# A conditioning product's sum over partitions: from two one-column TensorE products to 32x32 block transposes, row sums and one small product

## The chip, the cores and the metric

The kernel runs as one program on 1 core of one Trainium2 chip. The metric is the device time of one execution in microseconds (us); lower is better. The median of 3 runs of the kernel before is 2657.59 us (2654.68 to 2659.80).

## What is computed

Two transformer blocks in a row over 256 tokens of width 2048, all in float32. The first block has a gated delta-rule branch, a block attention branch and a gated feed-forward part; the second has a differential attention layer and a forgetting attention layer. What the change touches is the *conditioning* of the second block: a vector `c` gives shifts, scales and gates by three matrix-vector products.

```
def second_block(x, c, w_mod, b_mod, ..., kv_w_mod, kv_b_mod, ...):
    c_act = jax.nn.silu(c)                       # (1, 2048)
    for l in range(2):
        mod = c_act @ w_mod[l] + b_mod[l]        # (1, 2048) @ (2048, 6144)
        shift, scale, gate = jnp.split(mod, 3, axis=-1)
        h = x * (1.0 + scale[:, None]) + shift[:, None]
        ...
        x = layer_norm(DN_ALPHA * x + gate[:, None] * y, ln_g[l], ln_b[l])

def shared_kv(x, c_act, w_mod_kv, b_mod_kv, ...):
    mod = c_act @ w_mod_kv + b_mod_kv            # (1, 2048) @ (2048, 4096)
    ...
```

Together these products have 6144 + 6144 + 4096 = 16384 output columns, which is 32 chunks of 512 columns.

## The kernel before, in words

**The main line.** Sixteen large matrix products (`PLAN`: "qkv", "spill", "branch", "w_out", "ffn", "down", "v2" and so on) run one after the other. Each is cut into bodies, each body into units, 820 units in the loops in all. In one unit SyncE loads 512 KB of weights (`load`, L460) into a ring of 4 slots, ScalarE rounds them to float32r (`split`, L1254: `w_hi`), VectorE subtracts to get the remainder (`split`, L1858: `w_lo`), and TensorE does 12 products of 512 columns (L631 to L633, in `chunk`: operand high by weights high, high by low, low by high) or 24 of 256 columns (L654 to L656, in `across_chunk`). The counters `hi_done`, `lo_done` and `w_used` tie the engines together: ScalarE rounds the next slot when TensorE has used it.

**The conditioning product beside it.** One chunk of 512 columns takes 16 units of a body. In unit k SyncE loads a 128 x 512 piece of the conditioning weights (L484) and VectorE, behind its `split`, multiplies it by `c_act[:, k]` and adds it to `gemv_acc` (`gemv`, L1883; L1874 for k = 0). So after 16 units `gemv_acc` (128 x 512) holds, on each of the 128 partitions, a part of the sum, and what is left is the sum over partitions. Before, in unit k = 15, VectorE does the last step twice: once into `gemv_hi`, rounded to float32r (L1881), and once into `gemv_acc` (L1883); then it subtracts to get `gemv_lo` (L1888). Five units into the next body with a chunk (`mod_due` with lag 5), TensorE sums over partitions with a stationary column of ones, `ones_r[:, 0:1]`: two products of 512 columns, one for each half (`mod_reduce`, L664 and L665). The product "branch" has no chunk; the last chunk's sum is taken at the start of "g2". Two units later ScalarE copies the 1 x 512 row out of PSUM (`mod_copy`, L1279) and issues its DMA to `mods` in DRAM (L1282). `mods` is read back in two places, hundreds of us apart.

Waits around it: VectorE waits for `mod_stored` of the chunk before ahead of L1881 (`gemv_row` shares the bytes of `gemv_lo`); TensorE waits for `gemv_cut` (both halves written) in `mod_reduce`; ScalarE waits for `mod_sum`. The order on each engine is written out by hand.

**Work of other kinds between the units.** In "spill" (L631 to L633 with `u_hi`, `u_lo`) a generator `delta_net` puts the small products of the delta rule between units. One of these, L771 (`sums` <- `pick[:, ...]`, `sq`), is a plain float32 product with a stationary operand of 128 x 16; it is used for comparison below. Two others are L1165 (ones 128 x 128 times 2 columns) and L1221 (two transposes of 16 x 128 to 128 x 16). A plain float32 product shows in the trace as two MATMUL records, each with its LDWEIGHTS; a transpose or a float32r product as one.

Of the kernel before, what the change touches and what calls it, by code (L numbers as in the profile page):

```python
# [18 lines left out]
F32 = mybir.dt.float32  # L19
F32R = mybir.dt.float32r  # L20
ALU = mybir.AluOpType
ACT = mybir.ActivationFunctionType
AX = mybir.AxisListType
ds = bass.ds

P = 128
# [3 lines left out]
KD = D // P  # L30
# [6 lines left out]
H2 = 8  # L37
H3 = 16
COLS = 512
RING = 4  # L40
RMS_EPS = 1e-6
EPS = 1e-5
# [8 lines left out]
IDENT, ONES, CAUSAL, DIST = 0, 128, 256, 384  # L51
# [61 lines left out]
def block_kernel(nc, x, norm_mix_w, w_in, conv_w, a_log, dt_bias, gdn_o_norm_w, q_norm_w, k_norm_w,  # L113
# [5 lines left out]
    with ctx:  # L119

        at = [16512]

        def place(name, shape, dtype, offset=None):
            nbytes = 4 * int(np.prod(shape[1:]))
            if offset is None:
                offset = at[0]
                at[0] += (nbytes + 31) // 32 * 32
            return nc.alloc_sbuf_tensor_at(name, list(shape), dtype, offset=offset)

        raw = place("raw", [P, RING, 2, COLS], F32)  # L130
        w_hi = place("w_hi", [P, RING, 2, COLS], F32R)
        w_lo = place("w_lo", [P, RING, 2, COLS], F32R)
        xs = place("xs", [P, HALVES, D], F32)
        keep = place("keep", [P, KEEP_W], F32)
        cols = place("cols", [P, 3 * P], F32)
        modc = place("modc", [P, P], F32)
        small = place("small", [P, 464], F32)
        stage = place("stage", [P, 2, HALVES, COLS], F32)
        gemv_w = place("gemv_w", [P, 2, COLS], F32)
        gemv_acc = place("gemv_acc", [P, COLS], F32)  # L140
        gemv_hi = place("gemv_hi", [P, COLS], F32R)

        gemv_row = place("gemv_row", [P, COLS], F32, at[0])
        gemv_lo = place("gemv_lo", [P, COLS], F32R)
        ones_r = place("ones_r", [P, 2], F32R)
        region = at[0]
        K8 = 8 * 1024

# [116 lines left out]
        def sm(col, n=1, p0=0, p1=P):  # L265
            return small[p0:p1, col:col + n]
# [25 lines left out]
        ident = keep[:, IDENT:IDENT + P]  # L292
# [4 lines left out]
        bank = [ctx.enter_context(nc.psum_tensor(f"bank{b}", [P, COLS], F32)) for b in range(8)]  # L297
# [8 lines left out]
        mods = nc.dram_tensor("mods", (MOD_COLS // P, P), F32).ap()  # L306
# [41 lines left out]
        gemv_cut = sem("gemv_cut")  # L348
        gemv_step, mod_sum, mod_copied, mod_stored = sem("gemv_step"), sem("mod_sum"), sem("mod_copied"), sem("mod_stored")
# [3 lines left out]
        def signal(name):  # L353
            if name not in S:
                S[name] = sem(name)
            return S[name]
# [25 lines left out]
        for name, bodies, units, turns in PLAN:  # L382
            pr = products[name] = Product()
# [64 lines left out]
        def _(sp):  # L448
# [5 lines left out]
            def load(pr, i, j, w, pair, col):  # L454

                if not (isinstance(i, int) and pr.unit0 + i * pr.units + j < RING):

# [124 lines left out]
        def _(pe):  # L582
# [77 lines left out]
            def mod_reduce(n, b=MODB):  # L660


                pe.wait_ge(gemv_cut, n * 2 + 2)
                pe.matmul(bank[b][0:1, :], ones_r[:, 0:1], gemv_hi[:], start=True, stop=False)  # L664
                pe.matmul(bank[b][0:1, :], ones_r[:, 0:1], gemv_lo[:], start=False, stop=True).then_inc(mod_sum, 1)  # L665

            def mod_due(pr, i, j):

# [72 lines left out]
                    thin(ws_hi, ws_lo, u_hi, u_lo).then_inc(signal("logits"), 1)  # L741

            across_body("qkv", 0, u_hi, u_lo, first_due, {q: q + 1 for q in range(8)})
            pe.wait_ge(signal("ones_ready"), 1)
            for i in range(1, products["qkv"].bodies):
                across_body("qkv", i, u_hi, u_lo)

# [234 lines left out]
            pr = products["spill"]  # L982
# [6 lines left out]
            pr = products["branch"]  # L989
# [57 lines left out]
            pr = products["ffn"]  # L1047
# [144 lines left out]
            pr = products["v3"]  # L1192
# [51 lines left out]
        def _(act):  # L1244
# [31 lines left out]
            def mod_copy(n, b=MODB):  # L1276

                act.wait_ge(mod_sum, n + 1)
                act.copy(gemv_row[0:1, :], bank[b][0:1, :]).then_inc(mod_copied, 1)  # L1279
                act.wait_ge(mod_copied, n + 1)  # L1280
                dst = mods[ds(n * 4, 4), :].rearrange("r c -> (r c)").unsqueeze(0)
                act.dma_start(dst, gemv_row[0:1, :]).then_inc(mod_stored, 16)  # L1282

            def mod_due(pr, i, j):
                m = mod_part(pr, i, j, 7)
# [46 lines left out]
            def first_due(j):  # L1332
                if j in (1, 2):
                    operand_high(2 * j + 2)
                    operand_high(2 * j + 3)
                if j == 6:
                    act.wait_ge(signal("keep_in"), 16)
                    act.copy(ones_r[:], keep[:, ONES:ONES + 2]).then_inc(signal("ones_ready"), 1)
                    act.wait_ge(signal("ws_in"), 16)
                    act.wait_ge(signal("ws_zero"), 1)  # L1340
                    act.copy(ws_hi[:, :, 0:H1], ws_raw[:, :, 0:H1])
                    act.copy(ws_hi[:, :, 32:32 + H1], ws_raw[:, :, H1:2 * H1]).then_inc(signal("ws_high"), 1)
                if j == 8:
                    act.wait_ge(signal("cols_ready"), 1)
                    act.activation(c_act, cols[:, C_VEC:C_VEC + KD], ACT.Silu).then_inc(signal("c_ready"), 1)
# [221 lines left out]
            pr = products["spill"]  # L1567
# [8 lines left out]
            pr = products["branch"]  # L1576
# [42 lines left out]
            pr = products["ffn"]  # L1619
# [231 lines left out]
        def _(dve):  # L1851
# [8 lines left out]
            def gemv(pr, i, j):  # L1860

                if without_mod(pr, i):
                    return
                part = pr.units // pr.mods
                m, k = j // part, j % part
                if k >= KD:
                    return
                n = pr.mod0 + m
                c_k, w_k = c_act[:, k:k + 1], gemv_w[:, k % 2]
                dve.wait_ge(gemv_landed[k % 2], i * (pr.mods * 8 * KD) + (n * 8 * KD + 16 * (k // 2 + 1)))  # L1870
                if k == 0:
                    if not (isinstance(i, int) and i * pr.mods + n == 0):
                        dve.wait_ge(gemv_cut, i * (pr.mods * 2) + 2 * n)
                    dve.tensor_scalar(gemv_acc[:], w_k, c_k, None, ALU.mult).then_inc(gemv_step, 1)  # L1874
                    return
                dve.wait_ge(gemv_step, i * (pr.mods * KD) + (n * KD + k))
                if k == KD - 1:
                    if not (isinstance(i, int) and i * pr.mods + n == 0):

                        dve.wait_ge(mod_stored, i * (pr.mods * 16) + 16 * n)  # L1880
                    dve.scalar_tensor_tensor(out=gemv_hi[:], in0=w_k, scalar=c_k, in1=gemv_acc[:], op0=ALU.mult,  # L1881
                                             op1=ALU.add).then_inc(gemv_cut, 1)
                dve.scalar_tensor_tensor(out=gemv_acc[:], in0=w_k, scalar=c_k, in1=gemv_acc[:], op0=ALU.mult,  # L1883
                                         op1=ALU.add).then_inc(gemv_step, 1)
                if k == KD - 1:
                    dve.wait_ge(gemv_step, i * (pr.mods * KD) + (n * KD + KD))
                    dve.wait_ge(gemv_cut, i * (pr.mods * 2) + (2 * n + 1))
                    dve.tensor_tensor(gemv_lo[:], gemv_acc[:], gemv_hi[:].bitcast(F32), ALU.subtract).then_inc(gemv_cut, 1)  # L1888

            def body(name, i, drain, between=None, limit=UNITS, finish=None):  # L1890

# [75 lines left out]
            def first_due(j):  # L1967
                if j in (1, 2):
                    operand_low(2 * j + 2)
                    operand_low(2 * j + 3)  # L1970
                if j == 5:
                    dve.wait_ge(signal("cols_sum"), 1)
                    for n, r in enumerate(ROWS_USED):
                        first = 0 if n else KD
                        ins = dve.tensor_copy(cols[:, n * P + first:n * P + r], bank[SPARE][:, n * P + first:n * P + r])
                    ins.then_inc(signal("cols_ready"), 1)
                    dve.wait_ge(signal("cols_ready"), 1)
                if j == 6:
                    dve.tensor_scalar(sm(QNS), cols[:, QN_W:QN_W + 1], SCALE, None, ALU.mult)
                    for n in range(2):  # L1980
                        dve.tensor_tensor(sm(LAM + n), cols[:, LAMS + 2 * n:LAMS + 2 * n + 1],
                                          cols[:, LAMS + 2 * n + 1:LAMS + 2 * n + 2], ALU.mult)
                if j == 7:
                    dve.wait_ge(signal("ws_high"), 1)
                    dve.tensor_tensor(ws_lo[:, :, 0:H1], ws_raw[:, :, 0:H1], ws_hi[:, :, 0:H1].bitcast(F32), ALU.subtract)
                    dve.tensor_tensor(ws_lo[:, :, 32:32 + H1], ws_raw[:, :, H1:2 * H1], ws_hi[:, :, 32:32 + H1].bitcast(F32),
                                      ALU.subtract).then_inc(signal("ws_split"), 1)
# [311 lines left out]
            pr = products["branch"]  # L2299
# [55 lines left out]
            pr = products["ffn"]  # L2355
# [79 lines left out]
            pr = products["down"]  # L2435
# [321 lines left out]
```

## Time and profile before

| what | value |
|---|---|
| median of 3 runs | 2657.59 us (2654.68 to 2659.80) |
| the profiled execution's own time | 2654.59 us |
| its span, first to last instruction | 2652.8 us |
| mean granted TensorE clock | 0.992 of 2.4 GHz |
| PE (matmul) busy | 2586.1 us, 97% |
| DVE (VectorE) busy | 1796.1 us, 68% |
| ACT (ScalarE) busy | 1171.8 us, 44% |
| HBM | 227 GB/s mean over the span |

PE is TensorE's matmul side, PEld its weight loads, which overlap the matmuls. A matmul's duration in the trace (some 400 ns for 512 columns) holds its way through the array, so two that follow each other overlap; what one costs the engine is the distance between starts. The engine of the bottleneck is seen from its idle time, not from the share of busy time alone.

### The profile page before, as it was taken

How to read it: one execution, taken by the hardware profiler on the slowest of the kernel's cores; microseconds unless marked ns; L12 is line 12 of the kernel's file. 1: busy time of each engine (PE TensorE's matmuls, PEld its weight loads, DVE VectorE, ACT ScalarE, POOL GpSimd, SP SyncE). 2: the span in 40 equal slices, each digit the busy share in tenths (PEclk: the TensorE clock that was granted, in tenths of full speed). 3: DMA queues.
4: the chain of work that ended last, by engine and by line, in shares of the span. 5: the costliest groups of instructions: out<-in, count | busy, mean ns of one | idle time of the engine just before them, and what ended most of it. 6: DMA issues, size and time to landing. Idle time of an engine off the chain costs nothing.

```text
span 2652.8 us, 38762 instructions
## 1 busy us (share of the span) xinstructions
PE 2586.1 (97%) x14614; PEld 2175.5 (82%) x14614; DVE 1796.1 (68%) x2331; ACT 1171.8 (44%) x1475; POOL 0.2 (0%) x4
## 2 busy tenths in 40 slices
PE   8999999998999999999999999999999999999997
PEld 8977777777788778888887888899987778999885
DVE  6787676775567777777776666766786665545655
ACT  4454333454344544444443334333486344335642
POOL 0000000000000000000000000000000000000000
PEclk9999999999999999999999999999999999999998
DMA  7667676875768788888887777888845556665363
GB/s 209 195 234 249 218 229 208 276 254 192 250 209 269 260 270 269 275 274 271 272 275 246 251 249 254 278 273 272 252 141 182 181 167 183 182 215 165 123 224 125
DMA packets 313837, 604.69 MB, mean 228 GB/s; under 512 B 26670, under 2 KB 28724, under 8 KB 312028
## 3 DMA queue, kind: packets, MB, share of 16 engines
q1 hardware_dynamic: 301628, 571.59, 67.2%
q10 hardware_dynamic: 12064, 31.10, 3.2%
q8 instruction: 99, 1.62, 0.2%
q14 instruction: 46, 0.38, 0.0%
HBM read 591.98 MB, written 10.62 MB: 227 GB/s over the span
## 4 chain that ended last, share of the span: by engine, by line
PE 74%; DVE 2%; ACT 2%; issue 1%; DMA 1%; ACTq 0%; DVEq 0%; SPq 0%
PE bank L631 18%; PE bank L633 18%; PE bank L632 18%; PE bank L654 5%; PE bank L656 5%; PE bank L655 5%; PE bank L593 1%; PE bank L1091 1%; DVE w_lo L1858 1%; ACT w_hi L1254 0%; DMA raw<-in_w_branch_gdn 0%; PE bank L1102 0%; PE bank L1112 0%; PE bank L1088 0%; PE bank L1114 0%
## 5 line engine op out<-in xcount | busy, mean ns | idle before, releaser
L1858 DVE TENSOR_TENSOR w_lo<-raw,w_hi 128x1024 fp32r<-128x1024 f32 x820 | 1001.4, 1223 | 802.1 <-ACT w_hi L1254 801.0
L1254 ACT CAST w_hi<-raw 128x1024 fp32r<-128x1024 f32 x820 | 859.9, 1050 | 1371.7 <-PE bank L633 1028.2
L631 PE MATMUL bank<-w_hi,u_hi 128*128 128x512 f32 x1216 | 493.8, 406 | 3.1 <-DVE u_lo L1917 2.2
L632 PE MATMUL bank<-w_lo,u_hi 128*128 128x512 f32 x1216 | 483.8, 398 | 0.0
L633 PE MATMUL bank<-w_hi,u_lo 128*128 128x512 f32 x1216 | 483.2, 397 | 0.0
L1883 DVE SCALAR_TENSOR_TENSOR gemv_acc<-gemv_w,small,gemv_acc 128x512 f32<-128x512 f32 x480 | 357.8, 745 | 5.6 <-DMA gemv_w<-in_w_mod 5.2
L631 PE MATMUL bank<-w_hi,s_hi 128*128 128x512 f32 x768 | 311.1, 405 | 1.2 <-DVE w_lo L1858 1.1
L633 PE MATMUL bank<-w_hi,s_lo 128*128 128x512 f32 x768 | 304.6, 397 | 0.0
L632 PE MATMUL bank<-w_lo,s_hi 128*128 128x512 f32 x768 | 304.4, 396 | 0.0
L654 PE MATMUL bank<-s_hi,w_hi 128*128 128x256 f32 x1024 | 289.5, 283 | 0.0
L655 PE MATMUL bank<-s_lo,w_hi 128*128 128x256 f32 x1024 | 288.3, 282 | 0.0
L656 PE MATMUL bank<-s_hi,w_lo 128*128 128x256 f32 x1024 | 288.3, 282 | 0.0
L631 PEld LDWEIGHTS bank<-w_hi,u_hi 128*128 128x128 f32 x1216 | 230.3, 189 | 65.6 <-issue 8.1
L633 PEld LDWEIGHTS bank<-w_hi,u_lo 128*128 128x128 f32 x1216 | 230.3, 189 | 56.2
L632 PEld LDWEIGHTS bank<-w_lo,u_hi 128*128 128x128 f32 x1216 | 230.6, 190 | 51.5
L655 PEld LDWEIGHTS bank<-s_lo,w_hi 128*128 128x128 f32 x1024 | 193.2, 189 | 0.3
L656 PEld LDWEIGHTS bank<-s_hi,w_lo 128*128 128x128 f32 x1024 | 193.2, 189 | 0.0
L654 PEld LDWEIGHTS bank<-s_hi,w_hi 128*128 128x128 f32 x1024 | 192.0, 187 | 0.7 <-issue 0.3
L633 PEld LDWEIGHTS bank<-w_hi,s_lo 128*128 128x128 f32 x768 | 144.9, 189 | 35.3
L631 PEld LDWEIGHTS bank<-w_hi,s_hi 128*128 128x128 f32 x768 | 144.9, 189 | 34.8 <-DVE w_lo L1858 1.5
L632 PEld LDWEIGHTS bank<-w_lo,s_hi 128*128 128x128 f32 x768 | 145.2, 189 | 32.7
L631 PE MATMUL bank<-w_hi,hid_hi 128*128 128x512 f32 x352 | 140.0, 398 | 0.0
(356 smaller groups left out, 2903.5 us busy)
## 6 DMA issues: line engine op xcount, KB each, us to landing
gemv_w<-in_w_mod SPq DMA_DIRECT2D x384, 256.0 KB, 3.0
raw<-in_w_in SPq DMA_DIRECT2D x176, 512.0 KB, 4.5
raw<-in_a_w_in SPq DMA_DIRECT2D x128, 512.0 KB, 4.5
raw<-in_w_ffn_gate SPq DMA_DIRECT2D x88, 512.0 KB, 4.5
raw<-in_w_ffn_up SPq DMA_DIRECT2D x88, 512.0 KB, 4.1
raw<-in_w_ffn_down SPq DMA_DIRECT2D x88, 512.0 KB, 4.0
gemv_w<-in_kv_w_mod SPq DMA_DIRECT2D x128, 256.0 KB, 3.6
raw<-in_kv_w SPq DMA_DIRECT2D x64, 512.0 KB, 3.7
```

The lines of the kernel that those rows point to most:

```text
L593: ins = pe.transpose(b[:, f * T + th * P:f * T + (th + 1) * P], src(f, th), ident)
L631: pe.matmul(o, xh, w_hi[:, s, t], start=(k == 0), stop=False)
L632: pe.matmul(o, xh, w_lo[:, s, t], start=False, stop=False)
L633: ins = pe.matmul(o, xl, w_hi[:, s, t], start=False, stop=(k == 2 * units - 1))
L654: pe.matmul(o, wh, hi[:, k], start=(k == 0 and f % 2 == 0), stop=False)
L655: pe.matmul(o, wh, lo[:, k], start=False, stop=False)
L656: ins = pe.matmul(o, wl, hi[:, k], start=False, stop=(k == 2 * half - 1 and f % 2 == 1))
L1091: ins = pe.matmul(b[:, P:3 * P], queries_of[p][:, a, P:T], k_t[:, a, 0:T], start=True, stop=not mask)
L1254: act.copy(w_hi[:, s], raw[:, s]).then_inc(hi_done, 1)
L1858: dve.tensor_tensor(w_lo[:, s], raw[:, s], w_hi[:, s].bitcast(F32), ALU.subtract).then_inc(lo_done, 1)
L1883: dve.scalar_tensor_tensor(out=gemv_acc[:], in0=w_k, scalar=c_k, in1=gemv_acc[:], op0=ALU.mult, op1=ALU.add).then_inc(gemv_step, 1)
```

## The change

The split of `gemv_acc` into two float32r halves goes. In unit k = 15 VectorE does the last step once, transposes each 32 x 32 block of the 128 x 512 accumulator (`gemv_t`) and sums each run of 32 columns (`gemv_sums`, 128 x 16). Now partition 32a + j holds, in column b, the sum over the 32 partitions of quadrant a for the output column 32b + j. TensorE adds the four quadrants: one plain float32 product with `gemv_sums` (128 x 16) as the stationary operand and `quads` (128 x 32, a 1 where p mod 32 = column) as the moving one gives a 16 x 32 result, the chunk's 512 columns in order. `quads` is made once, from the identity, in unit 6 of the first body, by a VectorE row sum; the ScalarE copy that made `ones_r` there goes. ScalarE's copy and the DMA to `mods` handle 16 rows of 32 in place of 1 row of 512. VectorE's wait for `mod_stored` now stands before the row sum, behind the transpose. The small tiles take 2368 bytes a partition instead of 4128, so what is placed behind them moves down by 1760 bytes.

```
-        gemv_hi = place("gemv_hi", [P, COLS], F32R)
-
-        gemv_row = place("gemv_row", [P, COLS], F32, at[0])
-        gemv_lo = place("gemv_lo", [P, COLS], F32R)
-        ones_r = place("ones_r", [P, 2], F32R)
+        gemv_t = place("gemv_t", [P, COLS], F32)
+        gemv_sums = place("gemv_sums", [P, COLS // SQ], F32)
+        gemv_row = place("gemv_row", [P, SQ], F32)
+        quads = place("quads", [P, SQ], F32)
...
                 pe.wait_ge(gemv_cut, n * 2 + 2)
-                pe.matmul(bank[b][0:1, :], ones_r[:, 0:1], gemv_hi[:], start=True, stop=False)
-                pe.matmul(bank[b][0:1, :], ones_r[:, 0:1], gemv_lo[:], start=False, stop=True).then_inc(mod_sum, 1)
+                pe.matmul(bank[b][0:COLS // SQ, 0:SQ], gemv_sums[:], quads[:], start=True, stop=True).then_inc(mod_sum, 1)
...
-            pe.wait_ge(signal("ones_ready"), 1)
+            pe.wait_ge(signal("quads_ready"), 1)
...
                 act.wait_ge(mod_sum, n + 1)
-                act.copy(gemv_row[0:1, :], bank[b][0:1, :]).then_inc(mod_copied, 1)
+                act.copy(gemv_row[0:COLS // SQ], bank[b][0:COLS // SQ, 0:SQ]).then_inc(mod_copied, 1)
                 act.wait_ge(mod_copied, n + 1)
-                dst = mods[ds(n * 4, 4), :].rearrange("r c -> (r c)").unsqueeze(0)
-                act.dma_start(dst, gemv_row[0:1, :]).then_inc(mod_stored, 16)
+                dst = mods[ds(n * 4, 4), :].rearrange("r (q c) -> (r q) c", c=SQ)
+                act.dma_start(dst, gemv_row[0:COLS // SQ]).then_inc(mod_stored, 16)
...
-                if k == KD - 1:
-                    if not (isinstance(i, int) and i * pr.mods + n == 0):
-
-                        dve.wait_ge(mod_stored, i * (pr.mods * 16) + 16 * n)
-                    dve.scalar_tensor_tensor(out=gemv_hi[:], in0=w_k, scalar=c_k, in1=gemv_acc[:], op0=ALU.mult,
-                                             op1=ALU.add).then_inc(gemv_cut, 1)
                 dve.scalar_tensor_tensor(out=gemv_acc[:], in0=w_k, scalar=c_k, in1=gemv_acc[:], op0=ALU.mult,
                                          op1=ALU.add).then_inc(gemv_step, 1)
                 if k == KD - 1:
                     dve.wait_ge(gemv_step, i * (pr.mods * KD) + (n * KD + KD))
+                    dve.transpose(gemv_t[:], gemv_acc[:]).then_inc(gemv_cut, 1)
                     dve.wait_ge(gemv_cut, i * (pr.mods * 2) + (2 * n + 1))
-                    dve.tensor_tensor(gemv_lo[:], gemv_acc[:], gemv_hi[:].bitcast(F32), ALU.subtract).then_inc(gemv_cut, 1)
+                    if not (isinstance(i, int) and i * pr.mods + n == 0):
+                        dve.wait_ge(mod_stored, i * (pr.mods * 16) + 16 * n)
+                    dve.tensor_reduce(gemv_sums[:], gemv_t[:].rearrange("p (b c) -> p b c", c=SQ), AX.X, ALU.add).then_inc(
+                        gemv_cut, 1)
...
                 if j == 6:
+                    dve.wait_ge(signal("keep_in"), 16)
+                    dve.tensor_reduce(quads[:], ident.rearrange("p (q c) -> p c q", c=SQ), AX.X, ALU.add).then_inc(
+                        signal("quads_ready"), 1)
```

TensorE around the fourth chunk's sum, in "spill", before (the names behind the arrow are moving and stationary operand; the sizes are the output's):

```order
L633 MATMUL bank<-w_hi,u_lo 128x512
L664 MATMUL bank<-gemv_hi,ones_r 1x512
L665 MATMUL bank<-gemv_lo,ones_r 1x512
L631 MATMUL bank<-w_hi,u_hi 128x512
L632 MATMUL bank<-w_lo,u_hi 128x512
```

and after the change:

```order
L633 MATMUL bank<-w_hi,u_lo 128x512
L664 MATMUL bank<-quads,gemv_sums 16x32
L631 MATMUL bank<-w_hi,u_hi 128x512
L632 MATMUL bank<-w_lo,u_hi 128x512
```

Two instructions of 512 columns became one of 32, in the same place between the same neighbours.

VectorE in the last unit of the third chunk, before:

```order
L1858 TENSOR_TENSOR w_lo<-raw,w_hi 128x1024
L1881 SCALAR_TENSOR_TENSOR gemv_hi<-gemv_w,small,gemv_acc 128x512
L1883 SCALAR_TENSOR_TENSOR gemv_acc<-gemv_w,small,gemv_acc 128x512
L1888 TENSOR_TENSOR gemv_lo<-gemv_acc,gemv_hi 128x512
L1858 TENSOR_TENSOR w_lo<-raw,w_hi 128x1024
```

and after the change:

```order
L1855 TENSOR_TENSOR w_lo<-raw,w_hi 128x1024
L1874 SCALAR_TENSOR_TENSOR gemv_acc<-gemv_w,small,gemv_acc 128x512
L1878 STREAM_TRANSPOSE gemv_t<-gemv_acc 128x512
L1882 TENSOR_REDUCE gemv_sums<-gemv_t 128x16
L1855 TENSOR_TENSOR w_lo<-raw,w_hi 128x1024
```

Three instructions stay three, in the same place; two of them are of other kinds.

## Rows read from the trace of the kernel before

**Rows 1.** The page: busy time by engine; the granted clock in 40 slices.
```profile
PE 2586.1 (97%) x14614; PEld 2175.5 (82%) x14614; DVE 1796.1 (68%) x2331; ACT 1171.8 (44%) x1475; POOL 0.2 (0%) x4
...
PEclk9999999999999999999999999999999999999998
```

**Rows 2.** Busy time in stretches (us: length, busy us of each engine, clock, DMA).
```profile
160.00:700.00 540.00, 520.35 (x3388) 408.02 (x3386) 369.39 (x486) 240.84 (x310) 0.00 (x0) 0.98 0.72 237
700.00:1910.00 1210.00, 1204.15 (x5982) 1002.35 (x5983) 856.07 (x976) 499.47 (x536) 0.00 (x0) 1.00 0.80 261
```

**Rows 3.** Timeline, PE, around one chunk's sum (start us, duration us, engine, line).
```profile
376.99 0.40 PE L633 MATMUL bank<-w_hi,u_lo 128*128 128x512 f32 x1
377.22 0.40 PE L664 MATMUL bank<-gemv_hi,ones_r 128*1 128x512 f32 x1
377.46 0.40 PE L665 MATMUL bank<-gemv_lo,ones_r 128*1 128x512 f32 x1
377.69 0.39 PE L631 MATMUL bank<-w_hi,u_hi 128*128 128x512 f32 x1
```

**Rows 4.** Timeline, weight loads: of L664, and of L771.
```profile
376.99 0.08 PEld L664 LDWEIGHTS bank<-gemv_hi,ones_r 128*1 128x1 f32 x1
...
178.93 1.41 PEld L771 LDWEIGHTS bank<-sq,pick 128*16 128x16 f32 x8 [0.36 <-issue]
180.76 0.19 PEld L631 LDWEIGHTS bank<-w_hi,u_hi 128*128 128x128 f32 x1 [0.42 <-issue]
```

**Rows 5.** Timeline, PE, before and behind eight records of L771.
```profile
178.61 0.39 PE L633 MATMUL bank<-w_hi,u_lo 128*128 128x512 f32 x1
...
179.81 1.03 PE L771 MATMUL bank<-sq,pick 128*16 128x256 f32 x4
180.76 0.51 PE L631 MATMUL bank<-w_hi,u_hi 128*128 128x512 f32 x1
181.11 0.39 PE L632 MATMUL bank<-w_lo,u_hi 128*128 128x512 f32 x1
```

**Rows 6.** The instructions of L771 (count; duration ns min/median/max).
```profile
L771 PE MATMUL bank<-sq,pick x32: 376/379/518, 173.5 to 194.6; 128*16 128x256 f32 x32
```

**Rows 7.** Timeline, PE, around L1165.
```profile
1628.75 0.39 PE L633 MATMUL bank<-w_hi,hid_lo 128*128 128x512 f32 x1
1628.98 0.28 PE L1165 MATMUL bank<-small,keep 128*128 128x2 f32 x2
1629.12 0.48 PE L631 MATMUL bank<-w_hi,s_hi 128*128 128x512 f32 x1
1629.43 0.40 PE L632 MATMUL bank<-w_lo,s_hi 128*128 128x512 f32 x1
```

**Rows 8.** Timeline, PE, around L1221.
```profile
2257.66 0.29 PE L655 MATMUL bank<-s_lo,w_hi 128*128 128x256 f32 x1
2257.78 0.27 PE L656 MATMUL bank<-s_hi,w_lo 128*128 128x256 f32 x1
2257.99 0.29 PE L1221 MATMUL bank<-keep,zf_sb 16*128 16x16 f32 x2
2258.21 0.39 PE L654 MATMUL bank<-s_hi,w_hi 128*128 128x256 f32 x1
2258.43 0.28 PE L655 MATMUL bank<-s_lo,w_hi 128*128 128x256 f32 x1
```

**Rows 9.** Timeline, PE: what follows three of the 32 sums.
```profile
189.07 1.04 PE L771 MATMUL bank<-sq,pick 128*16 128x256 f32 x4
...
251.39 0.80 PE L897 MATMUL bank<-early,inv_t 64*64 64x64 f32 x20 [1.18 <-DVE inv_t L2225]
...
884.48 0.50 PE L631 MATMUL bank<-w_hi,u_hi 128*128 128x512 f32 x1 [2.15 <-DVE u_lo L1917]
```

**Rows 10.** Groups by line and shape, DVE (busy us, mean ns | idle before, releaser).
```profile
L1881 DVE SCALAR_TENSOR_TENSOR gemv_hi<-gemv_w,small,gemv_acc 128x512 fp32r<-128x512 f32 x32 | 23.9, 745 | 0.1
L1888 DVE TENSOR_TENSOR gemv_lo<-gemv_acc,gemv_hi 128x512 fp32r<-128x512 f32 x32 | 22.1, 692 | 2.2
L1874 DVE TENSOR_SCALAR gemv_acc<-gemv_w,small 128x512 f32<-128x512 f32 x32 | 15.4, 480 | 0.0
L2157 DVE TENSOR_REDUCE small<-work 128x1 f32<-128x256 f32 x32 | 13.1, 409 | 0.0
L2090 DVE TENSOR_REDUCE small<-o_sq 128x8 f32<-128x1024 f32 x2 | 2.4, 1206 | 0.0
```

**Rows 11.** Timeline, DVE: a reciprocal of 16 x 256; the last chunk's last instruction.
```profile
198.23 1.73 DVE L2069 RECIPROCAL gates<-gates 16x256 f32<-16x256 f32 x1
...
1911.08 0.69 DVE L1888 TENSOR_TENSOR gemv_lo<-gemv_acc,gemv_hi 128x512 fp32r<-128x512 f32 x1
```

**Rows 12.** Timeline, weight loads: the last chunk's sum.
```profile
1912.45 0.09 PEld L664 LDWEIGHTS bank<-gemv_hi,ones_r 128*1 128x1 f32 x1
```

**Rows 13.** Who waited for whom, DVE and ACT (us in total, times, longest us).
```profile
ACT w_hi L1254 <- PE bank L633: 1028.2, 567, 7.5
DVE w_lo L1858 <- ACT w_hi L1254: 801.0, 652, 6.1
```

More of the change, by code:

```diff
@@ L39 @@
 COLS = 512
+SQ = 32
 RING = 4
@@ L1336, in first_due @@
                 if j == 6:
-                    act.wait_ge(signal("keep_in"), 16)
-                    act.copy(ones_r[:], keep[:, ONES:ONES + 2]).then_inc(signal("ones_ready"), 1)
                     act.wait_ge(signal("ws_in"), 16)
```

## The prediction

> **What bounds the kernel now.** I read the page first: PE is busy 97% of the span, DVE 68%, ACT 44%, and the granted clock is at 0.9 or more of 2.4 GHz in all slices but the last [rows 1]. Then the stretches: from 700 to 1910 us, where 23 of the 32 chunks' sums lie (the 24th is at 1912), PE is busy 1204 of 1210 us, from 160 to 700 us, where the other eight lie, 520 of 540 [rows 2]. Then who waits for whom: the long waits are those of ACT for PE, 1028 us, and of DVE for ACT, 801 us [rows 13]. So TensorE sets the pace and hands it to the others; a microsecond taken from TensorE's stream is a microsecond of the kernel, unless TensorE has to stand right behind it, and work on VectorE or ScalarE costs nothing until it makes TensorE wait. That is why most of the working is about what one small product costs in the midst of TensorE's stream, and it has to be taken from distances between starts, since durations overlap.
>
> **What TensorE loses.** From L633 to the next L631 around a sum are 0.70 us, three steps of 0.233 us; two of them are L664 and L665 [rows 3]. Removed: 0.466 us a chunk, times 32 = 14.9 us.
>
> **What TensorE gains.** One plain float32 product, stationary operand 128 x 16, 32 columns. The trace has no such product of 32 columns, but it has L771 with the same stationary shape and 256 columns. From L633 to L632 around eight records of L771 are 181.11 - 178.61 = 2.50 us [rows 5]. Without them it would be two steps, 0.466, so they insert 2.03 us. Four of them take 1.03 us with one duration of 0.38 in it [rows 5, 6], so a record's step is (1.03 - 0.38) / 3 = 0.217 us, eight are 1.73, and 0.30 us is left over. The reason can be seen: the first weight load of L771 does not start behind the product before it, as that of L664 does (at 376.99, together with L633), but 0.32 us after L633's start, with an idle time before it that nothing in the profile explains, and the L631 that follows again loads late, 0.42 us idle [rows 4]. TensorE empties on both sides, at 0.32 - 0.23 = 0.09 us on entering, and then the first two weight loads of the large products are not hidden. The new product has two records, each 32/256 of 0.217 = 0.027 us. Inserted: 0.30 + 0.05 = 0.35 us a chunk. Net: 0.466 - 0.354 = 0.11 us, times 32 = 3.6 us.
>
> The bounds of this term come from two other small products. L1165 has a stationary operand of the full 128 x 128 and 2 columns: 1629.43 - 1628.75 = 0.68 us against 0.466, so it inserts 0.21 us; its weight load is early, nothing empties [rows 7]. By that the gain would be 0.25 us a chunk, 8.0 us. L1221, two transposes with 16 of 128 rows in use, stands among products of 256 columns, whose step is 0.12: 2258.43 - 2257.78 = 0.65 against 0.24, so 0.41 inserted, with two weight loads of 128 columns that ours does not have [rows 8]. By that the gain is 0.05 us a chunk, 1.7 us. I take L771's, since its form and its stationary shape are those of the new product.
>
> The Trainium skill, page "TensorEngine Tiling (Array Packing)", section "Key Properties", says that going from one tiling mode to another drains TensorE, with no price. L771's rows agree, at 0.30 us in all; L664's, whose stationary operand has one column, do not, as its weights load early [rows 4]. If the rule held for narrow products of every type, the pair removed would have paid as well and the gain would be up to 32 x 0.30 = 9.6 us more; the rows exclude that.
>
> **Corrections for neighbours.** Behind the first chunk's sum L771 follows at once [rows 9]: it pays the switch already, so 0.3 us more is gained there. Behind two others TensorE stands, 1.18 us for `inv_t` and 2.15 us for `u_lo` [rows 9], both from VectorE work released by products before the sum; their 0.1 us each goes into the wait. Together +0.1.
>
> **VectorE.** Removed a chunk: L1881, 0.745, and L1888, 0.692, in all 1.44 us. Added: a block transpose and a row sum of 128 x 512. The row sum is bounded by 0.41 for 256 columns and 1.21 for 1024; between them 1.04 ns a column, so 0.67 us [rows 10]. The transpose is not in the trace: from below 0.48 (L1874, the fastest pass over 128 x 512), from above the slowest per column that there is, a reciprocal of 256 columns at 1.73, so 3.5 for 512 [rows 10, 11]. I take 0.69, that of L1888, one plain pass, which is nearest in kind. Together 1.36 against 1.44: the same. The Trainium skill, page "Vector Engine (DVE) Microarchitecture Reference", section "The reshape front-end and per-opcode configuration", has the transpose sustain one element per cycle and lane; no row here shows it. The same skill's "VectorE: DVE Perf Modes", section "Rules for kernel authors", calls the row sum the slowest operation and advises restructuring; at 0.41 us for 256 columns it is no slower here than the 0.69 for 512 that it replaces, and neither would move TensorE.
>
> Who waits: the sums are ready five units ahead of TensorE's turn, some 14 us, except for the last chunk. There `gemv_lo` ends at 1911.77 [rows 11] and L664's weights load at 1912.45 [rows 12], a margin of 0.68 us; with the new pair the end is within 0.1 us of that. The wait for `mod_stored`, behind which the row sum and the next `split` are queued, is for a store issued eight units earlier, some 20 us. One row sum of some 0.3 us in unit 6 of the first body lies in VectorE's idle time [rows 13].
>
> **ScalarE, the DMA, the layout.** The copy of 16 x 32 in place of 1 x 512 can only be shorter, the store has 16 pieces of 128 bytes instead of one of 2048 and is read hundreds of us later; ScalarE waits 1028 us for TensorE [rows 13]. Nothing. Of the move by 1760 bytes no row says anything; nothing, with a spread in the range.
>
> **Sum.** 3.6 + 0.1 = 3.7 us less. The profiled execution's own time is 2654.59, so its like would be 2650.9; it stands 3.0 under the median of the runs, 2657.59, against which I predict 2653.9. What a measurement of this kernel tells from no change is 0.2%, 5.3 us, so this is the case "same", near its edge.
>
> **Rivals.**
> 1. *No emptying: the product costs what L1165's rows say.* For it: L664, which is as narrow, loads early [rows 4]. Against it: L664 is float32r, and L771, plain float32 and 128 x 16 like the new product, does not. Gain 8.0 us: 2649.6, faster. 15%.
> 2. *The transpose is slow.* If it takes 3.5 us, VectorE's chunk end grows by 2.7. TensorE then waits for it at the last chunk (2.7 - 0.7 = 2.0 us), and in the stretch from 160 to 700, where VectorE carries the delta rule's chain and TensorE already stands 20 us [rows 2], half of it may come through at each of eight chunks, 11 us. Less the 3.7 gained: +9, 2667, slower. In the 23 chunks between it hides in VectorE's idle time (354 of 1210 us). It cancels the gain from about 1.7 us a transpose on, and is over 0.2% from about 2.8 on. Against it: no pass over 512 columns in the trace takes over 0.75 us but for division. 12%.
> 3. *Stalls and clock fall otherwise.* The stretch from 160 to 700 and the one behind 1910 have waits between three engines, and the clock stood at 0.98 in the first [rows 2]; a shift of some tenths may lengthen or shorten these by 2 or 3 us. Either side, 2648 to 2660. 10%.
>
> **Chances.** The sum as worked out has 63%. Of that, with a spread of some 3 us from execution to execution (the three runs lie 5 us apart), 17 points fall beyond 0.2% faster, 44 within, 2 slower. Rival 1: 11 faster, 4 within. Rival 2: 8 slower, 4 within. Rival 3: 4 faster, 3 within, 3 slower. Sum: faster 0.32, same 0.55, slower 0.13. The range: 2647 takes in rival 1 with some spread; 2661 takes in a transpose of middling cost and L1221's price with the runs' spread. The likeliest case alone has 2650 to 2658.
>
> **What would show it.** Right: L664 (the new product) in two records per chunk, its first weight load about 0.32 us after L633's start with idle time before it, and about 0.82 us from that L633 to the second large product behind (0.47 + 0.35; before, four steps, 0.93). Wrong by rival 1: the weight load starts together with L633 and the same distance is about 0.68. Wrong by rival 2: the transpose's row says over 1.5 us, and TensorE waits for it at the last chunk. VectorE's busy time should be within 3 us of 1796, ScalarE's some 10 us lower, and the stretch from 900 to 1390 us, free of waits, shorter by 0.11 us for each of its sums.

## The result, and the profile after

| | us | runs |
|---|---|---|
| before | 2657.06 (2654.68 to 2659.80) | 4 |
| after | 2636.34 (2634.68 to 2636.89) | 4 |
| ratio | 0.9925, 95% interval 0.9913 to 0.9936 | |

The change gives 20.7 us, where 3.7 were forecast. The time lies 10.7 us below the low end of the range, and the case was called "same": the prediction was wrong. Below, 3.8 to 4.5 us of the gain turn out to be the sums, as forecast, and some 16 us to be the one item that was costed at nothing, the move of everything behind the small tiles.

The page of the changed kernel, first and clock lines:

```profile
span 2634.8 us, 38761 instructions
...
PE 2567.4 (97%) x14614; PEld 2169.4 (82%) x14614; DVE 1797.9 (68%) x2332; ACT 1157.7 (44%) x1474; POOL 0.2 (0%) x4
...
PEclk9999999999999999999999999999999999999998
```

The clock is as before [rows 1]. VectorE is 1.8 us busier, ScalarE 14.1 us less, TensorE 18.7 us less.

**The sum itself came out as forecast.** Timeline of PE and then of the weight loads around the chunk's sum near 925 us (start, duration, engine, line):

```profile
924.67 0.40 PE L633 MATMUL bank<-w_hi,u_lo 128*128 128x512 f32 x1
925.00 0.23 PE L664 MATMUL bank<-quads,gemv_sums 128*16 128x32 f32 x2
925.16 0.51 PE L631 MATMUL bank<-w_hi,u_hi 128*128 128x512 f32 x1
925.50 0.39 PE L632 MATMUL bank<-w_lo,u_hi 128*128 128x512 f32 x1
```
```profile
925.00 0.11 PEld L664 LDWEIGHTS bank<-quads,gemv_sums 128*16 128x16 f32 x2 [0.36 <-issue]
```

From L633 to the second large product behind are 925.50 - 924.67 = 0.83 us (forecast 0.82; before 0.93). The first weight load starts 0.33 us after L633, not together with it, with an idle time ahead of it that nothing explains: TensorE empties, as it does for L771 [rows 4].

The groups of the new instructions (busy us, mean ns | idle before), beside [rows 10]:

```profile
L1878 DVE STREAM_TRANSPOSE gemv_t<-gemv_acc 128x512 f32<-128x512 f32 x32 | 22.8, 712 | 1.1
L1882 DVE TENSOR_REDUCE gemv_sums<-gemv_t 128x16 f32<-128x512 f32 x32 | 22.0, 686 | 2.2
...
L664 PE MATMUL bank<-quads,gemv_sums 128*16 128x32 f32 x64 | 7.4, 198 | 0.0
L1278 ACT COPY gemv_row<-bank 16x32 f32<-16x32 f32 x32 | 5.4, 168 | 0.0
```

The transpose takes 0.71 us (taken: 0.69), the row sum 0.69 (0.67), and L664 has two records a chunk. So nothing of the arithmetic explains 20 us.

**Where the time went.** It is missing from TensorE's plain stream, far from any sum. Two rows of PE's timeline in "spill", sixty products of 512 columns apart (59 left out), before and after:

```profile
1071.72 0.39 PE L633 MATMUL bank<-w_hi,u_lo 128*128 128x512 f32 x1
...
1085.78 0.40 PE L633 MATMUL bank<-w_hi,u_lo 128*128 128x512 f32 x1
```
```profile
1071.68 0.40 PE L633 MATMUL bank<-w_hi,u_lo 128*128 128x512 f32 x1
...
1085.63 0.39 PE L633 MATMUL bank<-w_hi,u_lo 128*128 128x512 f32 x1
```

Before: 14.06 us, 234.3 ns from start to start. After: 13.95 us, 232.5 ns. The same code, the same clock, no wait, and each product comes 1.8 ns (0.8%) earlier. It is so ahead of the first sum as well, in the first large product, which has 256 columns. PE alone from 60 to 150 us, before and then after (length, busy us, records, clock, DMA share, GB/s):

```profile
60.00:150.00 90.00, 90.00 (x752) 1.00 0.66 207
```
```profile
60.00:150.00 90.00, 90.00 (x761) 1.00 0.66 208
```

The first sum comes at 184 us. What is in force before that is the placement of the tiles. I call **distance** the start of the area of the large tiles (`region`) less the start of the weight ring (byte 16512), modulo 256. Before it is 105952 - 16512, which is 96; after, 104192 - 16512, which is 128. In the products of 512 columns the large tiles hold the stationary operand and the ring the moving one (L633, `bank<-w_hi,u_lo`); in those of 256 columns it is the other way round (L655, `bank<-s_lo,w_hi` [rows 8]), so there stationary less moving is 256 minus this distance.

### The profile page after: what moved, and what is told of

Read it like the earlier page. It is cut to its first block, busy times and chain, and to the rows that moved or that the text cites. A ratio compares the mean times of both kernels' runs of the same rounds, so it can differ in the third digit from the quotient of the medians.

```text
span 2634.8 us, 38761 instructions
## 1 busy us (share of the span) xinstructions
PE 2567.4 (97%) x14614; PEld 2169.4 (82%) x14614; DVE 1797.9 (68%) x2332; ACT 1157.7 (44%) x1474; POOL 0.2 (0%) x4
## 4 chain that ended last, share of the span: by engine, by line
PE 91%; DVE 3%; ACT 2%; issue 2%; DMA 1%; ACTq 0%; DVEq 0%; SPq 0%
PE bank L631 22%; PE bank L633 21%; PE bank L632 21%; PE bank L656 6%; PE bank L654 6%; PE bank L655 6%; PE bank L593 1%; PE bank L755 1%; ACT w_hi L1253 1%; DVE w_lo L1855 1%; DVE gemv_acc L1874 1%; PE bank L1090 1%; DMA raw<-in_w_branch_gdn 0%; PE bank L781 0%; PE bank L1101 0%
## 5 line engine op out<-in xcount | busy, mean ns | idle before, releaser
L633 PE MATMUL bank<-w_hi,u_lo 128*128 128x512 f32 x1216 | 482.4, 397 | 0.0
L633 PE MATMUL bank<-w_hi,s_lo 128*128 128x512 f32 x768 | 303.6, 395 | 0.0
L655 PE MATMUL bank<-s_lo,w_hi 128*128 128x256 f32 x1024 | 289.7, 283 | 0.0
L633 PEld LDWEIGHTS bank<-w_hi,u_lo 128*128 128x128 f32 x1216 | 230.8, 190 | 54.2
L655 PEld LDWEIGHTS bank<-s_lo,w_hi 128*128 128x128 f32 x1024 | 192.9, 188 | 0.1
L633 PEld LDWEIGHTS bank<-w_hi,s_lo 128*128 128x128 f32 x768 | 145.1, 189 | 33.9
```

Source lines behind the costliest of these rows:

```text
L633: ins = pe.matmul(o, xl, w_hi[:, s, t], start=False, stop=(k == 2 * units - 1))
L655: pe.matmul(o, wh, lo[:, k], start=False, stop=False)
```

## The experiments

Where the expectations use letters: C has the arithmetic of the change give the whole gain; L64 has the address of the large tiles count by itself, modulo 64; R has the distance between the two areas count, M the distance modulo 256; T has the collision lie between TensorE's own two reads, moving operand and weights. "Step" is the distance between starts of successive large products, read as above over sixty products of 512 columns from 1072 us on, and over 48 of 256 columns.

### e1: the change's arithmetic at the old placement

```
+        at[0] += 1760
         region = at[0]
```

> The changed kernel with 1760 unused bytes in front of the large tiles, so that these stand where they stood before the change; the arithmetic is the change's. Seen so far: TensorE's step between two large products of 512 columns was 234.3 ns before and 232.4 ns after the change, in every stage, also ahead of the first sum; that is some 16 us of the 20.7. Theory L (the place of the operands in SBUF sets the step): the step goes back to 234.3 ns, the time to 2657.1 - 3.7 = 2653.4 us (2651 to 2656). Theory C (the new sums themselves set the step, by leaving TensorE in another state): the step stays at 232.4 ns, the time at 2636.3 us (2634 to 2639).

Measured: 2652.70 us (10 runs, 2648.45 to 2656.29) beside 2657.15 before (13 runs); ratio 0.999 (0.998 to 1.000). The step is 234.3 ns again (this kernel has one line more, so the large products' line numbers are one higher):

```profile
1071.62 0.40 PE L634 MATMUL bank<-w_hi,u_lo 128*128 128x512 f32 x1
...
1085.68 0.40 PE L634 MATMUL bank<-w_hi,u_lo 128*128 128x512 f32 x1
```

One body without waits, from a chunk's sum to the next one, splits the two parts. PE rows of the sum before, in e1, and after:

```profile
1069.38 0.40 PE L664 MATMUL bank<-gemv_hi,ones_r 128*1 128x512 f32 x1
...
1115.70 0.40 PE L664 MATMUL bank<-gemv_hi,ones_r 128*1 128x512 f32 x1
```
```profile
1063.87 0.23 PE L665 MATMUL bank<-quads,gemv_sums 128*16 128x32 f32 x2
...
1110.07 0.23 PE L665 MATMUL bank<-quads,gemv_sums 128*16 128x32 f32 x2
```
```profile
1062.58 0.23 PE L664 MATMUL bank<-quads,gemv_sums 128*16 128x32 f32 x2
...
1108.44 0.23 PE L664 MATMUL bank<-quads,gemv_sums 128*16 128x32 f32 x2
```

Before 46.32 us, e1 46.20, after 45.86. The new sum saves 0.12 us a chunk (forecast 0.11), times 32 = 3.8 us (over 22 of the sums among products of 512 columns the median distance from the large product before to the second behind is 0.928 us before and 0.816 in e1, also 0.11); the placement saves 0.34 in one body, which is 192 products times 1.8 ns. C falls.

### e2, e3, e4: 32 and 64 bytes more; the old kernel 32 bytes less

e2 is e1 with 32 in place of 1760, e4 with 64. e3 is the kernel before, with `ones_r` (8 bytes a partition, 32 in the layout) put into columns of `small` that nothing uses, so that the large tiles move down by 32 bytes:

```
+        small_at = at[0]
         small = place("small", [P, 464], F32)
...
-        ones_r = place("ones_r", [P, 2], F32R)
         region = at[0]
+        ones_r = place("ones_r", [P, 2], F32R, small_at + 4 * 184)
```

> The changed kernel with 32 unused bytes in front of the large tiles: they start at 32 mod 64 bytes, as before the change, but 1728 bytes lower. Theory L64 (what counts is whether the operands start at a multiple of 64 bytes): step 234.3 ns, time 2653.4 us (2651 to 2656). Theory L-far (what counts is the distance to the weights' ring, or a larger multiple than 64): step and time stay within 0.5 ns and 3 us of the changed kernel's 232.4 ns and 2636.3 us, or take a third value. Theory C: 232.4 ns, 2636.3 us.

> The kernel before with the large tiles 32 bytes lower, so that they start at a multiple of 64 bytes (the two-column tile of ones is put into unused columns of another tile); the arithmetic is that of before. Theory L64: step 232.4 ns, time 2657.1 - 17 = 2640 us (2637 to 2643). Theory C: step 234.3 ns, time 2657 us (2655 to 2659).

> The changed kernel with 64 unused bytes in front of the large tiles: still a multiple of 64 bytes, but no longer one of 128 or 256. Theory L64: step 232.4 ns, time 2636 us (2633 to 2640). A theory with 128 or 256 bytes in the place of 64: step 234.3 ns, time about 2653 us. Theory C: 232.4 ns, 2636 us.

Measured: e2 2639.21 (4 runs), ratio 0.9935 (0.9918 to 0.9951), step 233.3; e3 2640.08 (4 runs), the same ratio and interval, step 233.3; e4 2607.25 (1 run), step 229.0. e3 is the sharpest of the three: with all the old arithmetic in it, a move by 32 bytes gives 17.1 us, most of what the change gave. L64 falls: e2's address is no multiple of 64, and it did not go back to 234.3. e4 was a surprise to every theory: 29 us faster than the changed kernel by 64 bytes.

### e5, e6, e7: is it the address or the distance?

e6 moves the ring and all behind it up by 64 bytes, so the distance stays; that is its whole edit, shown here. e5 has the same line and keeps `region` at 104192: `gemv_row` goes to free bytes at the end, and 64 bytes of padding stand ahead of `region`. e7 is `at[0] += 128`.

```
-        at = [16512]
+        at = [16512 + 64]
```

> The changed kernel with the ring of weights (and the small tiles behind it) 64 bytes higher, the large tiles where the change has them. The runs so far: the place of the large tiles sets TensorE's step. Theory S (the large tiles' own place counts): step 232.4 ns and about 2636 us, as the changed kernel. Theory R (the distance between the ring and the large tiles counts, since one product reads one operand from each): another step than 232.4 ns.

> The changed kernel with everything, ring and large tiles, 64 bytes higher: the large tiles stand where e4 has them, the distance is that of the changed kernel. Theory S: e4's step of 228.9 ns, about 2607 us. Theory R: the changed kernel's 232.4 ns, about 2636 us.

> The changed kernel with 128 unused bytes in front of the large tiles. If the step falls further with the distance (0: 232.4, 32: 233.4, 64: 228.9 ns) it is below 228.9 ns and the time below 2607 us; if the place of 64 is a single good one, the step is back at 232 to 234 ns and the time at 2636 to 2653 us.

One run each, beside 2655.38 before: e5 2638.79, step 233.3; e6 2633.34, step 232.5; e7 2606.31, step 226.7. e6 has other addresses for both operands than the changed kernel and its step; e5 has the large tiles where the changed kernel has them, and the step of e3, whose distance modulo 256 is also 64. It is the distance that counts, as far as a ring moved by 64 bytes can tell. e7's two rows, sixty products apart:

```profile
1071.62 0.39 PE L632 MATMUL bank<-w_hi,u_hi 128*128 128x512 f32 x1
...
1085.22 0.39 PE L632 MATMUL bank<-w_hi,u_hi 128*128 128x512 f32 x1
```

13.60 us where before took 14.06, at the same clock.

### e8: a stationary operand of full width for the sum

`gemv_sums` becomes 128 x 128 with zeros in columns 16 to 127 (zeroed once); the product writes 128 x 32, of which 16 rows are used. It lies at the end of the memory, and `region` is padded to e4's place.

```
-        gemv_sums = place("gemv_sums", [P, COLS // SQ], F32)
+        gemv_sums = place("gemv_sums", [P, P], F32, 227712)
...
+        at[0] += 128
         region = at[0]
...
-                pe.matmul(bank[b][0:COLS // SQ, 0:SQ], gemv_sums[:], quads[:], start=True, stop=True).then_inc(mod_sum, 1)
+                pe.matmul(bank[b][:, 0:SQ], gemv_sums[:], quads[:], start=True, stop=True).then_inc(mod_sum, 1)
```

> e4's layout, with the small product's stationary operand widened to 128 x 128 (columns 16 to 127 are zeros, the output has 128 rows of which 16 are used). Theory D of the prediction (a stationary operand of 16 columns empties TensorE on both sides): the first weight load starts together with the product before, and what the sum inserts falls from 0.37 to about 0.21 us, in all 5 us less than e4's 2607. Without it: no gain, or a loss of up to 3 us by the longer weight loads.

Measured: 2599.67 (1 run), against e4's 2607.25; of these 7.6 us the sums below explain 4.5, the other 3 are about what single runs of one kernel differ by. PE and the weight loads around a sum of e8:

```profile
919.35 0.40 PE L634 MATMUL bank<-w_hi,u_lo 128*128 128x512 f32 x1
919.59 0.31 PE L665 MATMUL bank<-quads,gemv_sums 128*128 128x32 f32 x2
919.73 0.47 PE L632 MATMUL bank<-w_hi,u_hi 128*128 128x512 f32 x1
920.04 0.40 PE L633 MATMUL bank<-w_lo,u_hi 128*128 128x512 f32 x1
```
```profile
919.35 0.43 PEld L665 LDWEIGHTS bank<-quads,gemv_sums 128*128 128x128 f32 x2
```

The weights now load together with the large product before. From L634 to L633 are 0.69 us; less two steps of 0.229 that is 0.23 inserted, where the narrow one inserts 0.83 - 2 x 0.2325 = 0.37. So the emptying is the price of the narrow stationary operand, 0.14 us a chunk or 4.5 us in all. Rival 1 of the prediction, which did not happen, is thus built: its 0.21 of L1165 [rows 7] is nearly what such a product costs.

### e9, e10, e11: how the distance repeats

e9 pads by 224, e10 by 96, e11 by 160. e9's distance is 96 modulo 256, as before, but 1536 bytes less than before's.

> The changed kernel with 224 unused bytes in front of the large tiles. Theory M (the step depends on the distance between the ring and the large tiles modulo 256 bytes; so far 64: 233.3, 96: 234.3, 128: 232.4, 160: 233.4, 192: 228.9, 0: 226.8 ns for 512 columns): the distance is 96 modulo 256 as in the kernel before, though 1536 bytes less, so the step is 234.3 and 120.0 ns and the time 2653 us (2650 to 2656). Theory N (only the low end of the region, or the plain number of bytes, counts): the fast steps of 128 bytes stay, 227 ns and 2606 us.

> The changed kernel with 96 unused bytes in front of the large tiles: distance 224 modulo 256, between e4's 192 (228.9 ns) and e7's 0 (226.8 ns). Theory M does not say the value; it says that it is one value in every stage, ahead of the first sum too. Guess by the neighbours: 227 to 230 ns, 2600 to 2615 us.

> The changed kernel with 160 unused bytes in front of the large tiles: distance 32 modulo 256, between e7's 0 (226.8 ns) and e5's 64 (233.3 ns). Guess by the neighbours: 227 to 233 ns, 2606 to 2645 us; with e10 it closes the table of the eight residues.

One run each, beside 2654.23: e9 2649.67, steps 234.3 and 120.0; e10 2635.06, 233.3; e11 2634.57, 233.3. e9 gives back 13 of the 16 us and has both of the old steps; its time is 0.3 us below the expected range. The guess for e10 by its neighbours (227 to 230 ns, under 2615 us) missed, and so did e11's for the step: the values do not run evenly from one distance to the next. e9 and before lie 1536 bytes apart in distance, e3 and e5 1792, and each pair has the same steps; the largest number that divides both is 256, and 0 and 128 differ, as do 64 and 192, so it is the distance modulo 256. The table by distance, with the steps at 512 and 256 columns in ns:

| distance | kernels | 512 | 256 | us |
|---|---|---|---|---|
| 96 | before, e1, e9 | 234.3 | 120.0 | 2657.15, 2652.70, 2649.67 |
| 64 | e3, e5 | 233.3 | 117.7 to 117.9 | 2640.08, 2638.79 |
| 160 | e2 | 233.3 | 117.5 to 118.7 | 2639.21 |
| 224 | e10 | 233.3 | 118.3 | 2635.06 |
| 32 | e11 | 233.3 | 116.7, 117.7 | 2634.57 |
| 128 | after, e6 | 232.5 | 118.8, 120.0 | 2636.34, 2633.34 |
| 192 | e4 | 229.0 | 113.3, 117.9 | 2607.25 |
| 0 | e7 | 226.7 | 120.0 | 2606.31 |

### e12: the table in one kernel, behind the work

Behind the last product, ten products on the same operands for each of eight distances, made by shifting the stationary operand by 32 bytes (8 columns) at a time, at 512 and at 256 columns. They go to a bank that nobody reads; the ring is no longer written.

```
             second_out("o3", "f", out_turn_f)
+            for off in range(0, 64, 8):
+                for n in range(10):
+                    pe.matmul(bank[MODB][:], s2_lo[:, n, off:off + P], w_hi[:, n % 4, 0], start=True, stop=True)
```

> The changed kernel plus 160 products behind TensorE's last one, whose output nobody reads: for each of eight starts of the stationary operand, 32 bytes apart (distances 128, 160, 192, 224, 0, 32, 64, 96 modulo 256), ten products of 512 columns, then the same with 256 columns. ScalarE, VectorE and the DMAs no longer write the ring then. Theory T (the two reads of TensorE itself collide): the steps of 512 columns are, in this order, about 232.4, 233.4, 228.9, 233.3, 226.8, 233.3, 233.3, 234.3 ns. Theory E (TensorE collides with the others' writes): all eight are equal, and shorter.

Measured at 512 columns, the last eight steps of each ten, for distances 128, 160, 192, 224, 0, 32, 64, 96: 232.4, 233.5, 229.4, 233.4, 229.5, 233.1, 233.3, 233.9 ns. The order holds, 192 and 0 lowest, 96 highest, and seven of eight are within 0.5 of the large stream's; distance 0 has 229.5 in place of 226.7 (output was being stored then, but also during the ten at 64, which did not change).

At 256 columns: 118.4, 119.6, 117.8, 117.3, 119.1, 118.4, 113.4, 120.4. Here the large tiles hold the stationary operand, while the kernel's own products of 256 columns take it from the ring. By stationary less moving, 113.4 at 64 stands beside e4's 113.3 (distance 192 in the table), and 119.6 at 160 beside the 120.0 of before (distance 96); with 0, 32, 128, 192 and 224, seven of eight are within 0.9 ns of a step of the kernels. Only 96 is off, 120.4 against e2's 117.5 to 118.7. By the table's distance as it stands, 64 would be off by 4.3. That the sign counts is read from these numbers afterwards, and no run was made for it.

All engines during the products of 512 columns, during the tens at 64 and 96, and during the products of 256 columns (PE, PEld, DVE, ACT, POOL, clock, DMA share, GB/s):

```profile
2616.00:2634.00 18.00, 18.00 (x79) 14.57 (x78) 13.72 (x15) 0.49 (x2) 0.00 (x0) 1.00 0.29 117
2630.00:2634.00 4.00, 4.00 (x19) 3.23 (x18) 0.00 (x0) 0.00 (x0) 0.00 (x0) 1.00 0.52 214
2634.40:2643.50 9.10, 9.10 (x80) 9.10 (x79) 0.00 (x0) 0.00 (x0) 0.00 (x0) 1.00 0.00 0
```

In the last stretch no other engine and no DMA works at all, and the step still goes by the distance, from 113.4 to 120.4 ns. In the middle one VectorE and ScalarE are idle, and 64 and 96 keep their 233.3 and 233.9. So theory E, a collision with the writes of others, is not needed for the dependence. What is left in both areas is TensorE's own reads of weights and of the moving operand; that these two hold each other up (T) is inferred, since no trace shows a single read. The Trainium skill, page "SBUF — State Buffer", section "Who interferes with whom", gives TensorE two read ports, one for the moving operand and one for weight loads, and calls them independent. By that no distance should matter; the steps of 226.7 to 234.3 ns disagree, as far as T is the reading.

### e13, e14: the best version, timed

The wide stationary operand at distance 0 (e13) and at 192 (e14; the program of e8 again, with rounds).

> The wide stationary operand of e8 with e7's layout (distance 0 modulo 256, steps of 226.8 and 120.0 ns). If the two add up: e7's 2606.3 less 5 to 7 us, about 2600 us, 0.978 of the time before. If they do not: 2604 us or more.

> e8's kernel again, with rounds: distance 192 modulo 256, steps of 228.9 ns, and 113.3 or 117.8 ns for 256 columns. Expected as e8: 2600 us (2597 to 2603), the same as e13 within 3 us.

Measured beside 2656.27 (9 runs): e13 2600.79 (5 runs, 2599.30 to 2601.37), ratio 0.9790 (0.9777 to 0.9803); e14 2599.81 (4 runs, 2598.58 to 2600.25), ratio 0.9786 (0.9771 to 0.9801). The two can't be told apart: distance 0 has the faster step at 512 columns, 192 at 256. Both beat the changed kernel by some 36 us and the kernel before by some 56. PE alone from 900 to 1300 us, in the kernel before and in e13:

```profile
900.00:1300.00 400.00, 400.00 (x1747) 1.00 0.84 273
```
```profile
900.00:1300.00 400.00, 400.00 (x1810) 1.00 0.86 281
```

The same 400 us hold 1810 of TensorE's products where they held 1747.

## Why the prediction was wrong

**The step that failed** is the last sentence of "ScalarE, the DMA, the layout": "Of the move by 1760 bytes no row says anything; nothing, with a spread in the range." It was worth 16.4 us (e1 against after, 2652.7 - 2636.3). The steps give the same size: the program has 7776 large products of 512 columns, times 1.8 ns = 14.0 us, and 4224 of 256, whose mean step fell from 120.0 to about 119.2, 3.4 us; together 17.4. That these two agree within 1 us is partly luck. In the traces e1's lag behind the changed kernel grows by 1.8 ns a product from the 4000th to the 6800th large product (990 to 1670 us), as it should, but from the 1200th to the 3600th (180 to 900 us) it does not grow at all, and the two profiled executions end 11.9 us apart, with e1's the fastest of its ten. The same shows in e7, where the steps at 512 columns alone would give 7776 x 7.6 = 59 us less than e1 and 46 came: over the 2000 products from 180 to 800 us, where TensorE also stands for others [rows 2], it gains 5.5 us of 15. The step is thus what the plain stream gives, and an upper bound where there are waits.

The premise was that a product's step belongs to its shape. The trace of one kernel can't contradict it, for the placement is the same throughout. But the unknown could have been bounded: the path that sets the end is 12000 products long, 7776 x 0.2343 + 4224 x 0.120 = 2329 us, so 1% of their step is 23 us, over four times what a measurement can tell. An unknown that acts on the whole of a bottleneck wants a wide range, even where nothing in the trace speaks for it; this one got no number, and no rival.

**The sum on TensorE: right.** Forecast 0.11 us a chunk, shown 0.12; in all 3.7, against 3.8 from the body and 4.5 from the medians of e1 and before (interval of that ratio: 0 to 5 us). L771 was the right model: late weight load, 0.37 us inserted against 0.354. The bounds were right as well: L1165's price is what e8 pays. e8 also shows the reading behind it, that the emptying goes with the narrow plain float32 stationary operand. That it is the change of tiling rather than the width in some other way is argued, not shown.

**VectorE: right.** Transpose 0.71 and row sum 0.69 us; busy 1797.9, forecast within 3 of 1796. At the last chunk the row sum ends at 1896.33 and L664's weights load at 1897.20, a margin of 0.87 us where it was 0.68:

```profile
1895.64 0.69 DVE L1882 TENSOR_REDUCE gemv_sums<-gemv_t 128x16 f32<-128x512 f32 x1
```
```profile
1897.20 0.11 PEld L664 LDWEIGHTS bank<-quads,gemv_sums 128*16 128x16 f32 x2 [0.36 <-issue]
```

Rival 2, the slow transpose, did not occur. The Trainium skill's "VectorE: DVE Perf Modes", section "Rules for kernel authors", calls the row sum the slowest operation; at 686 ns it matches the 692 of the subtraction that it replaced [rows 10], so there was nothing to restructure.

**ScalarE and the DMA: right.** ScalarE is 14.1 us less busy (forecast some 10), its wait for TensorE is 1034 us where it was 1028 [rows 13], and nothing waits for the store.

**The stretches (rival 3).** From 700 to 1910 us TensorE is busy 1207.35 us, from 160 to 700 it is 516.15:

```profile
160.00:700.00 540.00, 516.15 (x3378) 405.92 (x3378) 373.14 (x490) 239.33 (x312) 0.00 (x0) 0.99 0.72 237
700.00:1910.00 1210.00, 1207.35 (x6045) 1010.06 (x6045) 863.74 (x994) 493.80 (x547) 0.00 (x0) 1.00 0.81 263
```

Beside [rows 2] TensorE stands 4 us more in the first and 3 less in the second, with clocks 0.01 apart, and since the after kernel is earlier at any time the stretches don't hold quite the same work. The 4 us are slightly more than the 2 or 3 that the rival allowed, but the two all but cancel, and 1 us is too small for the gain.

**What the forecast tests could not catch.** "The stretch from 900 to 1390 us shorter by 0.11 us for each of its sums" came out as 0.46 in one body: the one forecast that would have shown the error at once.

## What to carry to other kernels

Where one engine is busy all the time, read its step (start to start, over fifty or more equal instructions in a stretch without waits) before costing anything else, and read it again after: here a per cent of it outweighed everything that was costed. A change that alters the size of small allocations also moves the large operands behind them, so test it with the placement held fixed, by padding, before crediting its arithmetic; then walk the placement by itself, 32 bytes at a time over 256, and keep the best. In TensorE's stream a plain float32 product with a narrow stationary operand cost the emptying around it, and filling it up to 128 columns with zeros was cheaper by 0.14 us each.

## What the runs showed of the hardware that was not expected

- The step of float32r products of 512 columns depends on the distance of the two operands in memory modulo 256: 226.7 ns at 0, 229.0 at 192, 232.5 at 128, 233.3 at 32, 64, 160 and 224, 234.3 at 96. Over the kernel this is 46 us (e1 against e7). It stays when no other engine and no DMA works (e12, at 256 columns). Why these values are fast and those slow is open, as are distances between the multiples of 32.
- At 256 columns, where ring and large tiles change roles, the order is another (113.3 to 120.0), and one placement can have two paces: in the changed kernel the step is 120.0 from 1708 to 1725 us and 118.7 from there to 1891, and it changes where a sum's product empties TensorE, at 1725.04. That suggests that the pace also depends on how weight reads and moving reads are offset in time. It is not tested, and it may be why e12's ten products differ from the stream at distance 0.
- Kernels with the same distance and arithmetic lie up to 3 us apart (e1 and e9; after and e6), while their steps at 512 columns agree to 0.1 ns. At 256 columns after and e6 agree up to 2240 us and then run at 120.0 and 118.7, which is over 1 us of their 3. The single runs are used here by their steps and not by such differences.
